# Eight of sixteen stretches of attention probabilities turned in blocks, and a pair's block moves divided between ScalarE and VectorE

## The reference

```python
def trunk(x, ...):
    u = rmsnorm(h, norm_mix_g[i])
    mix = neighbourhood_attention(u, na_w_qkv[ia], na_rpb[ia], na_w_o[ia])
    h = h + mix.astype(h.dtype)
    u = rmsnorm(h, norm_ffn_g[i])
    h = h + expert_choice_ffn(u, router_w[i], moe_w_gate[i], moe_w_up[i], moe_w_down[i])
    return rmsnorm(h, final_norm_g)
```

## Time and profile before

| | |
|---|---|
| median of 3 runs | 1520.35 us (1520.34 to 1520.6) |
| profiled execution | 1520.91 us, its span 1519.1 us |
| TensorE (PE) busy | 1505.3 us, 99% of the span |
| VectorE (DVE) busy | 1316.2 us, 87% |
| ScalarE (ACT) busy | 1250.3 us, 82% |
| granted TensorE clock | 0.999 |

### The profile page before, as it was taken

The page is one execution under the profiler, slowest core; times in us unless marked ns, Lnnn a source line. Parts: engine busy times, 40 slices in busy tenths (PEclk is TensorE's granted clock), DMA queues, the critical chain, the costliest instruction groups (busy, mean ns, idle before and its releaser), DMA issues.

```text
span 1519.1 us, 22067 instructions
## 1 busy us (share of the span) xinstructions
PE 1505.3 (99%) x7738; PEld 1217.5 (80%) x7738; DVE 1316.2 (87%) x1415; ACT 1250.3 (82%) x1491; POOL 330.1 (22%) x154
## 2 busy tenths in 40 slices
PE   9999999999999999999999999999999999999997
PEld 7888878888863888888888888888888888888886
DVE  7684786785865899999999999999999999999988
ACT  6756656546453799999999999999999999999997
POOL 0000001000022232242322523233242322420103
PEclk9999999999999999999999999999999999999999
DMA  9633447433476999999999999999999999999998
GB/s 346 193 137 124 154 140 265 124 125 111 151 248 225 395 420 391 415 400 404 407 406 405 397 411 391 398 407 399 412 388 404 405 393 414 395 414 382 387 396 349
DMA packets 156407, 498.59 MB, mean 328 GB/s; under 512 B 10880, under 2 KB 36608, under 8 KB 156352
## 3 DMA queue, kind: packets, MB, share of 16 engines
q1 hardware_dynamic: 144624, 461.54, 77.6%
q0 software_dynamic: 9280, 31.07, 6.6%
q10 hardware_dynamic: 2448, 5.25, 1.3%
HBM read 473.70 MB, written 20.97 MB: 326 GB/s over the span
## 4 chain that ended last, share of the span: by engine, by line
PE 89%; ACT 3%; DVE 3%; DMA 2%; issue 2%; SPq 0%; POOLq 0%; POOL 0%; ACTq 0%; DVEq 0%
PE ps L2093 76%; PE ps L2142 4%; PE ps L2149 2%; ACT w_high L1253 2%; PE ps L2258 2%; DVE w_rest L1404 2%; PE ps L2193 1%; PE ps L2414 1%; DMA raw<-w_gate 1%; PE ps L2199 1%; DMA u_rows<-arena 1%; ACT arena L1224 1%; DMA raw<-w_qkv 1%; PE ps L2696 0%; PE ps L2410 0%
## 5 line engine op out<-in xcount | busy, mean ns | idle before, releaser
L1404 DVE TENSOR_TENSOR w_rest<-raw,w_high 128x2048 fp32r<-128x2048 f32 x212 | 477.9, 2283 | 40.9 <-ACT w_high L1253 25.1
L1253 ACT CAST w_high<-raw 128x2048 fp32r<-128x2048 f32 x184 | 352.1, 1915 | 17.6 <-PE ps L2093 14.7
L2093 PE MATMUL ps<-w_high,xt_high 128*128 128x512 f32 x984 | 305.2, 390 | 0.7 <-DVE w_rest L1404 0.6
L2093 PE MATMUL ps<-w_rest,xt_high 128*128 128x512 f32 x984 | 304.3, 389 | 0.0
L2093 PE MATMUL ps<-w_high,xt_rest 128*128 128x512 f32 x984 | 304.2, 389 | 0.0
L2093 PEld LDWEIGHTS ps<-w_high,xt_high 128*128 128x128 f32 x984 | 184.1, 188 | 41.5 <-DVE w_rest L1404 2.4
L1404 DVE TENSOR_TENSOR w_rest<-early,w_high 128x2048 fp32r<-128x2048 f32 x90 | 204.4, 2286 | 13.3 <-ACT w_high L1253 13.3
L2093 PEld LDWEIGHTS ps<-w_high,xt_rest 128*128 128x128 f32 x984 | 184.7, 188 | 38.4
L2093 PEld LDWEIGHTS ps<-w_rest,xt_high 128*128 128x128 f32 x984 | 184.7, 188 | 38.3
L1404 DVE TENSOR_TENSOR w_rest<-raw_more,w_high 128x2048 fp32r<-128x2048 f32 x92 | 206.0, 2274 | 4.7 <-ACT w_high L1253 4.7
L1224 ACT COPY arena<-arena 32x256 f32<-32x256 f32 x464 | 187.3, 404 | 10.6
(11 more groups left out here) (319 smaller groups left out, 2304.0 us busy)
## 6 DMA issues: line engine op xcount, KB each, us to landing
raw<-w_down SPq DMA_DIRECT2D x64, 1024.0 KB, 8.8
raw<-w_gate SPq DMA_DIRECT2D x62, 1024.0 KB, 8.2
raw<-w_up SPq DMA_DIRECT2D x62, 1024.0 KB, 9.6
raw_more<-w_down SPq DMA_DIRECT2D x32, 1024.0 KB
early<-w_down SPq DMA_DIRECT2D x32, 1024.0 KB, 8.0
raw_more<-w_gate SPq DMA_DIRECT2D x31, 1024.0 KB
raw_more<-w_up SPq DMA_DIRECT2D x31, 1024.0 KB
early<-w_gate SPq DMA_DIRECT2D x31, 1024.0 KB, 9.5
```

Of the source, the lines that this page charges most:

```text
L1253: nc.scalar.copy(w_high[:, i % SLOTS, :], src).then_inc(high_done, 1)
L1404: nc.vector.tensor_tensor(w_rest[:, j, :], src, w_high[:, j, :].bitcast(F32), ALU.subtract).then_inc(rest_done, 1)
L2093: done = nc.tensor.matmul(out, lhs, rhs, start=start and part == 0, stop=stop and part == 2)
```

## The change

A table now names the stretches that are turned in blocks: pair 0 of the first group, pair 1 of the second, and both of the third, 8 of 16 over both trunks. In the two new ones of each trunk the block moves are divided: ScalarE copies those of the pair's first call as soon as that call is transposed, 16 copies of 32x256, and VectorE those of the second call, 16 copies of 32x256. TensorE's turn, and the PSUM copies behind it, go in these stretches, and `values` waits for the copies instead.

With it the order of VectorE changes around these stretches: the biases of calls 2 and 3 come ahead of `split_ot`; the two transposes and 16 copies come in; a rest of weights (v, 3) moves to the end of the second group; that of (w, 3) moves from the third group into the last group, ahead of the biases of calls 2 and 3; in trunk 0's last group the rest of the next trunk's q moves down to the last but one `add_out` of w, and that of its k down behind `split_x`, ahead of the first `copy_h`. In trunk 0's third group `mean_square` comes behind the rests of q and k. ScalarE makes the other sequence's root, and then loads the exponential's table, ahead of the second `split_ot` of that group. Two semaphores become one with two counts.

```diff
 def by_blocks(n):
-    return n % HEADS // GROUP % 2 == 0 and n % GROUP < PAIRED
+    return (n % HEADS // GROUP, n % GROUP // PAIRED) in BY_BLOCKS
...
+BY_BLOCKS = ((0, 0), (1, 1), (2, 0), (2, 1))
+SHARED_MOVES = ((1, 1), (2, 1))
...
+        def half_block_of(n, half):
+
+            into, of = block_of(n)
+            return into[:, 1 - half, :], of[:, 1 - half, :]
@@ ScalarE @@
+            def share_moves(A):
+
+                act.wait_ge(pt_dve, A + 1)
+                for n in range(MOVES):
+                    nc.scalar.copy(*half_block_of(n, 0)).then_inc(pt_moved, 1)
@@ VectorE @@
+            def share_moves(A):
+
+                dve.wait_ge(pt_dve, A + PAIRED)
+                for n in range(MOVES):
+                    nc.vector.tensor_copy(*half_block_of(n, 1)).then_inc(pt_carried, 1)
...
                 if by_blocks(A + hh):
-                    pe.wait_ge(pt_moved, MOVES * (turned_by_blocks(A) // PAIRED + 1))
+                    shared = (g, p) in SHARED_MOVES
+                    if shared and half:
+                        pe.wait_ge(pt_carried, MOVES * (shared_before(A + hh - half) // PAIRED + 1))
+                    else:
+                        pe.wait_ge(pt_moved, MOVES * (turned_by_blocks(A + hh - half) // PAIRED + 1))
...
-                turn_probabilities(A, 2)             # TensorE, second and third group
...
                 exponentials(A, 3)                   # ScalarE, third group
+                share_moves(A + PAIRED)
+                cast_qk(b, 3, "q", 0)
+                cast_qk(b, 3, "k", 0)
                 if b == 0:
                     next_piece(8)
                     root(1)
-                copy_pt(A, 2)
-                copy_pt(A, 3)
-                cast_qk(b, 3, "q", 0)
-                cast_qk(b, 3, "k", 0)
+                    nc.scalar.preload_act_table(ACT.Exp)
                 split_ot(A, 2, 1)
...
                 if picking:                          # VectorE, last group
                     merge(0)
-                if b + 1 < TRUNKS:
-                    rest_pair(b, "q", GROUPS)
+                rest_pair(b, "w", 3)
                 biased(A, b, g, 2)
...
                 if b + 1 < TRUNKS:
-                    rest_pair(b, "k", GROUPS)
+                    rest_pair(b, "q", GROUPS)
                 add_out(b, g, "w", 7, 8)
...
                     split_x(b + 1, 0, 2)
+                    rest_pair(b, "k", GROUPS)
                 copy_h(b, 0)
```

More of the change, by code:

```diff
@@ L119, in by_blocks, with shared_before @@
 def by_blocks(n):
-    return n % HEADS // GROUP % 2 == 0 and n % GROUP < PAIRED
+    return (n % HEADS // GROUP, n % GROUP // PAIRED) in BY_BLOCKS
 def turned_whole(n):
     return sum(not by_blocks(m) for m in range(n))
+def shared_before(n):
+    return sum((m % HEADS // GROUP, m % GROUP // PAIRED) in SHARED_MOVES for m in range(n))
 def turned_by_blocks(n):
@@ L502, in head_count, with block_of @@
             return HEADS * b + GROUP * g
+        def block_of(n):
+            a, c = n % QUARTERS, n // QUARTERS
+            queries, keys = slice(a * QUARTER, (a + 1) * QUARTER), slice(c * QUARTER, (c + 1) * QUARTER)
+            return (arena[keys, 0:TILES:TILES - 1, a * WIN:(a + 1) * WIN], arena[queries, 1:TILES - 1, c * WIN:(c + 1) * WIN])
+        def half_block_of(n, half):
+            into, of = block_of(n)
+            return into[:, 1 - half, :], of[:, 1 - half, :]
         @block.sync
@@ L905, in move_pt @@
                 for n in range(MOVES):
[L906 to L909, removed]
+                    nc.scalar.copy(*block_of(n)).then_inc(pt_moved, 1)
+            def share_moves(A):
+                act.wait_ge(pt_dve, A + 1)
+                for n in range(MOVES):
+                    nc.scalar.copy(*half_block_of(n, 0)).then_inc(pt_moved, 1)
             def cast_qk(b, g, what, m):
@@ L1490, in turn_blocks_pt @@
                 dve.wait_ge(norm_done, TILES * (A + hh + 1))
-                probabilities = scores[hh].rearrange("p i (c b j) -> p b (i c) j", c=2, b=QUARTERS)
-                nc.vector.transpose(pt[hh], probabilities).then_inc(pt_dve, 1)
+                probabilities = scores[hh % 2].rearrange("p i (c b j) -> p b (i c) j", c=2, b=QUARTERS)
+                nc.vector.transpose(pt[hh % 2], probabilities).then_inc(pt_dve, 1)
+            def share_moves(A):
+                dve.wait_ge(pt_dve, A + PAIRED)
+                for n in range(MOVES):
+                    nc.vector.tensor_copy(*half_block_of(n, 1)).then_inc(pt_carried, 1)
             def normalise_rows(A, hh):
@@ L1645, in second_group @@
                 add_out(b, g, "w", 7, 8)
-                split_ot(b, g, 0)
                 biased(A, b, g, 2)
                 biased(A, b, g, 3)
+                split_ot(b, g, 0)
+                normalise_rows(A, 2)
+                turn_blocks_pt(A, 2)
+                normalise_rows(A, 3)
+                turn_blocks_pt(A, 3)
+                copy_q(b, g, 0)
+                share_moves(A + PAIRED)
                 rest_pair(b, "v", 2)
[L1650 to L1653, removed]
                 copy_k(b, g, 0)
-                copy_pt(A, 2)
-                copy_pt(A, 3)
                 rest_qk(b, g + 1, "q", 0)
@@ L1681, in third_group @@
                 add_out(b, g, "w", 4, 8)
-                split_ot(b, g, 0)
                 biased(A, b, g, 2)
                 biased(A, b, g, 3)
+                split_ot(b, g, 0)
+                normalise_rows(A, 2)
+                turn_blocks_pt(A, 2)
+                normalise_rows(A, 3)
+                turn_blocks_pt(A, 3)
+                copy_q(b, g, 0)
+                share_moves(A + PAIRED)
+                copy_k(b, g, 0)
                 rest_pair(b, "w", 2)
-                normalise_rows(A, 2)
-                normalise_rows(A, 3)
+                rest_qk(b, g + 1, "q", 0)
+                rest_qk(b, g + 1, "k", 0)
                 if b == 0:
                     mean_square(1)
[L1690 to L1696, removed]
                 split_ot(b, g, 1)
@@ L2637, in _ @@
                 _, last = whole_gate_up(late_xt, kc, 2, slice(0, CAP), slice(CAP, P), kc == 0, kc == KC - 1)
-            last.then_inc(third_used, 1)
+            last.then_inc(third_mm, 1)
             places()
```

18 lines of the change are left out of this document (9 added, 9 removed).

## The result

The change makes the kernel slower: 1527.72 us, the median of 6 runs (1525.89 to 1529.1), against 1520.46 for the kernel before in 6 runs; the ratio is 1.0048, 95% interval 1.0038 to 1.0058. The forecast was 1524.2: the right side, and the measured time lies in the wide range (1517.0 to 1528.5), but at the very end of the forecast's own (1521.8 to 1527.7), and the loss is 7.3 us and not 3.8. The profiled execution took 1527.26, with a span of 1525.5 (before 1519.1).

What follows compares the result with a forecast made beforehand. TensorE was taken as the bound, busy 1030.41 of 1039.00 us behind 480 and critical through the front. Terms -4.8 + 4.4 + 1.3 + 1.2 + 1.7 = +3.8; 1520.91 + 3.8 - 0.56 = 1524.2 us, range 1517.0 to 1528.5.

Steps and rivals of the forecast that it cites:

- Turns, -4.8: Four turns removed from TensorE, one in the second and third group of each trunk, at 1.2 us each: -4.8 us.
- Price of a copy, 0.31: VectorE's sixteen 32x256 copies per new stretch: 0.31 us each from start to start, 4.9 for sixteen; ends 0.14 and 0.44.
- The cheap: Rival: VectorE's copies at or under 0.2 us each, so the third group's wait falls to 0.4; +0.3, 1520.6; chance 0.26.
- the dear rival: VectorE's copies at 0.44 us each, as out of PSUM, with waits in third and second groups; +11.2, 1531.5; chance 0.08.
- Third group, +2.2 in each trunk: VectorE's chain of 18.5 us exceeds TensorE's window of 16.3, so TensorE waits 2.2 before the last group's scores; +4.4 together.
- Second group, none: The same VectorE chain against a window of 19.05 us: 0.5 to spare, so no wait of TensorE.
- Last group of trunk 0, +1.3: ScalarE's root and table loads make the biases 1.7 us later relative to the scores; 0.4 to spare at the turn: +1.3.
- Tails, +1.2 and +1.7: Moved rests on VectorE delay the first router tile in trunk 0, +1.2 us, and bank emptying in trunk 1's last group, +1.7.
- The step that failed: TensorE bounds the front too, so each microsecond it waits or saves there moves the rest by as much.

## Why the prediction was right in kind and short in size

**Turns, -4.8.** Right: the windows of the second groups, which hold only a saved turn and the copies, shrink by 0.96 and by 1.23; with the 0.20 of wait the first is 1.16.

**Price of a copy, 0.31.** Right: 0.315. The cheap and the dear rival both fall with it. That the duration, 0.284, is just the middle of the two bounds is luck: no row fixed it between 0.21 and 0.35. By the Trainium skill (VectorE: DVE Perf Modes, "Two Vector instructions with no wait between them") these copies are held till the one before has ended, and the trace bears it out in all four groups of sixteen: 0.284 long, 0.315 apart.

**Third group, +2.2 in each trunk.** Right, 2.49 and 2.52: the chain was 18.6 where the sum had 18.5, and the window 0.2 shorter. **Second group, none.** Right but for 0.20 in trunk 0.

**Last group of trunk 0, +1.3.** The term was right and didn't show: the biases began 183.05 - 179.04 = 4.01 behind the scores, as forecast, but TensorE came to its turn 1.5 later at its lower clock and no longer waited. In the kernel as made the 1.3 is no part of the loss; the slow clock's 1.5 stands in its place. With the clock kept, the wait appeared, 0.65 in one kernel and 0.24 + 1.28 in another.

**Tails, +1.2 and +1.7.** Right in size, 1.18 and 1.88; with the rests moved both went, though in trunk 0 the rest's new place cost 0.5.

**The step that failed** is the first one, that a microsecond that TensorE waits moves the rest by as much. A wait of 2.3 to 2.5 us took 1.5 to 1.6 more with it, through the clock, in every profile that had it (three kernels, both trunks); those of 1.04 in the same place, and of 0.93 and 1.12 in the tails, did not. The profile of before could not price it, as no such wait stood in its front, but the forecast could have named it: it put an idle TensorE of 2.2 us in a program whose clock was 1.00 in all of the front. That is +3.05 over both trunks, less the 1.3 that it covered: 3.8 + 1.75 is 5.55, and the 1.0 that is left to 6.6 in the front is 0.6 in the third groups and 0.2 each in the second groups and the tails.

**The same step, for what is saved.** That a microsecond saved on TensorE moves the rest by as much holds even less: the three kernels with 1.8 to 2.6 us less in the front in their first profiles measured between 0.5 more and 0.9 less than the kernel before. The traces show three places where it goes, each in some executions: the gather (waits of 0.23 to 1.43, against 0.49 and 0.91 in the two profiles of before), the last store in one of the three kernels (1.55 ahead of it; 0.68 to 0.84 in the others), and a stall of ScalarE in one profile. What share each has in the median stays open, since runs of one kernel differ by up to 3 us and only one or two of each were profiled.

## What to carry to other kernels

Where one engine is saturated, a wait put on it is priced by its length only while it is short: look in the view by stretches for what the clock does behind the longest idle time that the change makes. Work moved onto the engine that makes the operands of the critical one must be summed over the whole window up to the wait, and the order inside that window decides: here 2.2 us of weights that could be made elsewhere stood ahead of the operands that were waited for. And when a run's time fits one theory, read its waits too: a wait taken away may uncover another that it had hidden. A front made shorter is no gain yet: three kernels show it in the trace, and none in the time.

## What was not expected of the hardware

- The granted clock fell behind waits of TensorE of 2.30 to 2.52 us, in three kernels and both trunks of each, and came back about 3.5 us later; behind waits of 0.93 to 1.28 in the front, and of 1.43 at the gather, it stayed at 1.00. The runs of the kernel after that took longest (1528.6, 1529.1) had the lowest mean clock, 0.994, the shortest (1525.89) the highest, 0.998.
- Before the last indirect store POOL took 0.68 to 1.78 us with nothing to wait for, in kernels that don't differ there. It goes by the kernel more than by the execution: 0.84 and 0.85 in the two profiles of before, 0.68 and 0.80 in the two of the kernel with the second group alone, and 1.49 to 1.78 in the kernel after and four kernels made from it. The cause is open.
